# A hybrid decoder block: last down-projection step by token halves, the memset of the sums moved, residual in three pieces, other banks for the memory values

## The reference, cut to what matters

```python
x = x + rmsnorm(merged @ w_o[l], g_post_mix[l])
h2 = rmsnorm(x, g_pre_ffn[l])
u = causal_dwconv(h2 @ w_up[l], conv_w[l], conv_b[l])      # 2 x 5632 columns, 3 taps over the tokens
u_gate, u_val = jnp.split(u, 2, axis=-1)
f = (jax.nn.gelu(u_gate, approximate=True) * u_val) @ w_down[l]
x = x + rmsnorm(f, g_post_ffn[l])                          # rmsnorm: v * rsqrt(mean(v*v) + 1e-6) * g
```

## Time and profile before

| | |
|---|---|
| median of 3 runs | 1752.44 us |
| the profiled execution | 1752.13 us |
| its span, first to last instruction | 1749.8 us |
| granted TensorE clock, mean | 0.998 of full speed |
| PE / DVE / ACT / POOL busy | 98% / 63% / 47% / 2% |
| bytes over the DMA queues | 327.77 MB, 187 GB/s |

### The profile page before, as it was taken

One profiled execution on the slowest core, in us unless ns is written; L12 is line 12 of the kernel. 1 busy time (PEld: TensorE's weight loads), 2 busy tenths in 40 slices (PEclk: granted clock), 3 DMA queues, 4 the chain that ended last, 5 costly groups with the idle time before them and its releaser, 6 DMA issues.

```text
span 1749.8 us, 26499 instructions
## 1 busy us (share of the span) xinstructions
PE 1710.7 (98%) x9645; PEld 1499.8 (86%) x9645; DVE 1095.5 (63%) x1426; ACT 817.0 (47%) x1107; POOL 42.9 (2%) x49
## 2 busy tenths in 40 slices
PE   6999999999999999999999999999999999999997
PEld 6998999999878888888888788888888888888885
DVE  5644557666566454564565667776676676676676
ACT  5433335444434434434444555455454455454453
POOL 0000000000031000000000100000000000000000
PEclk9999999999999999999999999999999999999999
DMA  8755458545465666666647555666666666666663
GB/s 260 228 176 185 143 147 275 159 144 156 150 199 165 191 197 192 208 201 193 190 166 252 182 166 188 191 190 187 190 193 192 189 190 188 191 192 191 193 188 115
DMA packets 246146, 327.77 MB, mean 187 GB/s; under 512 B 12727, under 2 KB 167464, under 8 KB 245544
## 3 DMA queue, kind: packets, MB, share of 16 engines
q1 hardware_dynamic: 246056, 326.47, 60.2%
HBM read 321.71 MB, written 3.67 MB: 186 GB/s over the span
## 4 chain that ended last, share of the span: by engine, by line
PE 94%; DVE 2%; DMA 2%; ACT 1%; issue 0%; SPq 0%; DVEq 0%; POOL 0%; ACTq 0%; POOLq 0%
PE bank L1295 18%; PE bank L1285 15%; PE bank L1286 15%; PE bank L1287 15%; PE bank L1299 9%; PE bank L1259 4%; PE bank L1261 4%; PE bank L1260 4%; PE bank L1272 1%; PE bank L1274 1%; PE bank L1273 1%; DMA wraw<-in_w_in 1%; DVE wlo L795 1%; ACT whi L527 1%; DMA wraw<-in_w_o 0%
## 5 line engine op out<-in xcount | busy, mean ns | idle before, releaser
L795 DVE TENSOR_TENSOR wlo<-wraw,whi 128x1024 fp32r<-128x1024 f32 x588 | 722.6, 1234 | 481.5 <-ACT whi L527 479.5
L527 ACT ACTIVATE whi<-wraw 128x1024 fp32r<-128x1024 f32 x588 | 621.4, 1060 | 719.2 <-PE bank L1287 395.0
L1295 PE MATMUL bank<-hx,whi 128*128 128x512 f32 x1376 | 344.5, 392 | 0.0
L1295 PEld LDWEIGHTS bank<-hx,whi 128*128 128x128 f32 x1376 | 248.0, 189 | 44.9
L1299 PEld LDWEIGHTS bank<-hx,wlo 128*128 128x128 f32 x1376 | 187.7, 190 | 13.4
L1299 PE MATMUL bank<-hx,wlo 128*128 128x256 f32 x1376 | 191.9, 282 | 0.0
L1285 PE MATMUL bank<-whi,hx 128*128 128x512 f32 x448 | 175.7, 392 | 0.0
L1287 PE MATMUL bank<-whi,hx 128*128 128x512 f32 x448 | 174.4, 389 | 0.0
L1286 PE MATMUL bank<-wlo,hx 128*128 128x512 f32 x448 | 174.3, 389 | 0.0
L1285 PE MATMUL bank<-whi,r_hi 128*128 128x512 f32 x416 | 162.2, 390 | 0.0
L1286 PE MATMUL bank<-wlo,r_hi 128*128 128x512 f32 x416 | 162.0, 389 | 0.0
(11 more groups left out here) (241 smaller groups left out, 2071.6 us busy)
## 6 DMA issues: line engine op xcount, KB each, us to landing
wraw<-in_w_in SPq DMA_DIRECT2D x200, 512.0 KB, 3.6
wraw<-in_w_up SPq DMA_DIRECT2D x176, 512.0 KB, 4.4
wraw<-in_w_down SPq DMA_DIRECT2D x88, 512.0 KB, 4.2
wraw<-in_w_mem_kv SPq DMA_DIRECT2D x32, 512.0 KB, 4.3
wraw<-in_w_o SPq DMA_DIRECT2D x32, 512.0 KB, 4.4
wraw<-in_w_br_mem SPq DMA_DIRECT2D x16, 512.0 KB, 4.1
wraw<-in_w_br_nsa SPq DMA_DIRECT2D x16, 512.0 KB, 4.5
wraw<-in_w_br_ret SPq DMA_DIRECT2D x16, 512.0 KB, 4.3
```

The source lines that it names most:

```text
L527: nc.scalar.activation(whi[:, c], wraw[:, c], ACT.Copy).then_inc(hi_done, 1)
L795: V.tensor_tensor(wlo[:, c], wraw[:, c], whi[:, c].bitcast(F32), ALU.subtract).then_inc(lo_done, 1)
L1295: T.matmul(ps[UP_PAIRS[j][t]][:, :], whi[:, c, k, t * P:(t + 1) * P], hx[:, :, k0 + k, :], start=first and k == 0, stop=False, skip_group_ ...
```

## The change

- The last down step goes by token halves: all 2048 columns of tokens 0 to 127 in the banks 0, 1, 6, 7, then those of tokens 128 to 255 in 2, 3, 4, 5. All eight weight chunks have to stay, so the last four go to the buffers `m_hi` and `m_lo`, which are free by then (`kept`). VectorE's additions, ScalarE's squares, the mean, power, residual sum and stores follow half by half; the power is of one column each.
- GpSimd's memset of `M` waits for the last split tile of the norm instead of for `x2`.
- The residual ahead of the norm is made and squared in pieces of 1024, 512 and 512 channels.
- "mv" uses bank pair (2, 7) first and (0, 1) second; group 0 waits for no pair, group 1 for what was emptied before the phase.
- In retention VectorE multiplies by the decay ahead of the first weight split instead of behind it.

```diff
+X2_PARTS = [(0, 1024), (1024, 1536), (1536, 2048)]
-OUT_PARTS = [(0, 0, 512), (0, 512, 1024), (1, 0, 1024), (1, 1024, 512), (0, 1536, 512), (1, 1536, 512)]
+OUT_PARTS = [(0, 0, 1024), (0, 1024, 1024), (1, 0, 512), (1, 512, 512), (1, 1024, 512), (1, 1536, 512)]
-NEW_PAIRS = ("mv", "rg")
+LAST_BANKS = ((0, 1, 6, 7), (2, 3, 4, 5))
...
+        def kept(buf, c):
+            return (m_hi, m_lo)[buf].rearrange("p k s -> p (k s)")[:, 1024 * c:1024 * (c + 1)]
...                                             # GpSimd
-            pool.wait_ge(s_x2, 2 * TT)
+            pool.wait_ge(s_trl, 2 * KT)
             nc.gpsimd.memset(arena[:, A_M:A_M + 4096], 0.0).then_inc(s_f0, 1)
-            rstd(6)
+            half_rstd(6, 0)
+            half_rstd(7, 1)
...                                             # ScalarE, hi()
+                if isinstance(q, int) and q == DN_LAST:
+                    nc.scalar.activation(kept(0, c), wraw[:, c].rearrange("p k n -> p (k n)"), ACT.Copy).then_inc(hi_done, 1)
+                    return
...                                             # ScalarE, norm
             row_squares(1, 1)
+            row_squares(1, 2)
...                                             # ScalarE, last step
-            for g in range(4):
-                for t in range(TT):
-                    act.wait_ge(s_dn, 4 + 8 * (STEPS - 1) + 2 * g + t + 1)
+            for t in range(TT):
+                for g in range(4):
+                    act.wait_ge(s_dn, 4 + 8 * (STEPS - 1) + 4 * t + g + 1)
...                                             # VectorE, "mv"
-                ch.add(V.tensor_copy(by_head(A_MV + 1024 * i, 0), ps[PAIRS[i][0]][:, :]...))
-                dve.sem_inc(evac[i], 1)
+                ch.add(V.tensor_copy(by_head(A_MV + 1024 * i, 0), ps[PAIRS[1 - i][0]][:, :]...))
+                dve.sem_inc(evac[1 - i], 1)
...                                             # VectorE, retention
-                    ahead(q, (0,))
                     dve.wait_ge(r_i, r + 1)
                     ...                         # the two products with the decay
-                    ahead(q, (1,))
+                    ahead(q, (0, 1))
...                                             # VectorE, last step
+            ahead(Q0["dn"])
+            for t in range(TT):
+                for g in range(4):
+                    dve.wait_ge(s_dl, 4 * t + g + 1)
+                    f = M[:, t, 512 * g:512 * (g + 1)]
+                    V.tensor_tensor(f, ps[LAST_BANKS[t][g]][:, :], f, ALU.add).then_inc(s_dn, 1)
+                    if g:
                         times_gain(g - 1, t)
-            mean_square(4, 4, (s_sq, 16), lambda: [times_gain(3, t) for t in range(TT)], 6)
-            ch.wait()
-            for part in OUT_PARTS:
-                post(M, *part, s_fin)
+                dve.wait_ge(s_sq, 8 + 4 * t + 4)
+                half_square(t, 0, 4, 0)
+                times_gain(3, t)
+                ch.wait()
+                dve.wait_ge(s_rstd, 7 + t)
+                for part in OUT_PARTS:
+                    if part[0] == t:
+                        post(M, *part, s_fin)
...                                             # TensorE, group()
+                if phase == "mv":
+                    for b in range(2 * i):
+                        pe.wait_ge(evac[b], G0[phase] // 2)
...
+                pair = PAIRS[(i + (phase == "mv")) % 2]
...                                             # TensorE, last step
+            def last_down(q, s, u):
+                pe.wait_ge(s_al, s + 1)
+                for b in range(2):
+                    pe.wait_ge(evac[b], up_group(s + 1))
+                for t in range(TT):
+                    if t:
+                        pe.wait_ge(s_dn, 8 * s + 4)
+                    for g in range(4):
+                        o = ps[LAST_BANKS[t][g]][:, :]
+                        for c in range(2):
+                            n = 4 * (g // 2) + 2 * (g % 2) + c
+                            if t == 0:
+                                pe.wait_ge(lo_done, 4 * q + n + 1)
+                            ...                 # chunks 0 to 3 from whi, wlo, chunks 4 to 7 from kept
+                            for k in range(2):
+                                ...
+                                T.matmul(o, xh, vh[:, k, :], start=c == 0 and k == 0, stop=False)
+                                T.matmul(o, xh, vl[:, k, :], start=False, stop=False)
+                                e = T.matmul(o, xl, vh[:, k, :], start=False, stop=c == 1 and k == 1)
+                        e.then_inc(s_dl, 1)
```

More of the change, by code:

```diff
@@ L695, in row_squares @@
             def row_squares(t, h):
[L697 to L699 removed]
+                act.wait_ge(s_x2, 3 * t + h + 1)
+                own = slice(*X2_PARTS[h])
+                nc.scalar.activation((r_hi, r_lo)[t][:, own], X[:, t, own], ACT.Square, accum_out=sq[:, 1, t, h:h + 1]).then_inc(s_ssq, 1)
             def half_hi(t, pairs):
@@ L711, in _ @@
             group_squares(3, 0)
-            row_squares(0, 0)
-            row_squares(0, 1)
+            for h in range(3):
+                row_squares(0, h)
             act.wait_ge(pe_done, 4 * WO_LAST + 4)
@@ L790, in lo @@
                 dve.wait_ge(hi_done, 4 * q + (c + 1))
-                if isinstance(q, int) and q == WO_LAST:
+                if isinstance(q, int) and q == DN_LAST:
+                    V.tensor_tensor(kept(1, c), wraw[:, c].rearrange("p k n -> p (k n)"), kept(0, c).bitcast(F32),
+                                    ALU.subtract).then_inc(lo_done, 1)
+                elif isinstance(q, int) and q == WO_LAST:
                     V.tensor_tensor(held(1, c), wraw[:, c].rearrange("p k n -> p (k n)"), held(0, c).bitcast(F32),
@@ L1131, in _ @@
             dve.wait_ge(s_rstd, 3)
[L1132 to L1135, removed]
+            for h in range(3):
+                residual(0, h)
+            dve.wait_ge(s_ssq, 2 * 2 * TT + 3)
+            half_square(0, 6, 3, 1)
             dve.wait_ge(s_rstd, 4)
@@ L1147, in _ @@
             residual(1, 1)
+            residual(1, 2)
             half_lo(0, (4, 5))
-            dve.wait_ge(s_ssq, 2 * 2 * TT + 4)
-            half_square(1, 6, 2, 1)
+            dve.wait_ge(s_ssq, 2 * 2 * TT + 6)
+            half_square(1, 6, 3, 1)
             half_lo(0, (6, 7))
@@ L1386, in group @@
             def group(q, chunks, i, phase, x_, between={}, tiles_ready=None):
-                for b in range(2):
-                    if b == i % 2 or (i == 0 and phase in NEW_PAIRS):
-                        pe.wait_ge(evac[b], G0[phase] // 2 + i // 2)
+                if phase == "mv":
+                    for b in range(2 * i):
+                        pe.wait_ge(evac[b], G0[phase] // 2)
+                else:
+                    for b in range(2):
+                        if b == i % 2 or (i == 0 and phase == "rg"):
+                            pe.wait_ge(evac[b], G0[phase] // 2 + i // 2)
+                pair = PAIRS[(i + (phase == "mv")) % 2]
                 for c in range(chunks):
@@ L1394, in group @@
                         pe.wait_ge(tiles_ready[0], tiles_ready[1] + c + 1)
-                    chunk_w(q + c // 4, c % 4, PAIRS[i % 2], *x_, 2 * c, c == 0, c == chunks - 1)
+                    chunk_w(q + c // 4, c % 4, pair, *x_, 2 * c, c == 0, c == chunks - 1)
                     if c in between:
@@ L1694, in _ @@
                 down(q + 4, s, s % 2)
-            down(Q0["dn"], STEPS - 1, 0)
+            last_down(Q0["dn"], STEPS - 1, 0)
 def constants():
```

29 lines of the change are left out of this document (15 added, 14 removed).

## The result

| | before | after |
|---|---|---|
| median of the runs beside each other | 1752.61 us (4 runs, 1752.35 to 1753.65) | 1743.04 us (4 runs, 1742.29 to 1743.83) |
| the profiled execution | 1752.13 us | 1743.83 us |
| its span | 1749.8 us | 1741.4 us |

The ratio is 0.9941, 95% interval 0.9928 to 0.9953: 9.6 us less.

A forecast was written before the change was run, and what follows sets the result against it. TensorE, busy 98% of the span, was taken as the bound, leaving only its waits and the tail. Gains of 1.0 + 2.3 + 1.05 + 3.6 = 7.95 us off 1752.13, plus 0.3 for the median, gave 1744.5 us; range 1743.2 to 1747.9.

The forecast's parts named there:

- rival A: Behind the norm: the memset holds up the weight splits, TensorE loses 3.3 us, 1747.8 us; chance 0.1.
- Rival B: Last down step: VectorE becomes the bound, 0.3 to 1.5 us of tail gain lost, about 1745.5 us; chance 0.15.
- D: Last down step, first pass: a TensorE pause drops its clock to 1.2 GHz, 10.9 us more, 1755.4 us; chance 0.02.
- stalls in retention: Retention outputs: with the decay first, TensorE's waits go; 1.8 + 3 x 0.16 = 2.3 us gained.
- the stores' backlog: Tail: the transfer backlog of some 0.4 us at the end goes; 0.25 us of it counted as gain.
- "mv": Start of the memory values: the other bank pair spares group 0 its wait for a copy; 1.0 us gained.
- rival C: "mv" and retention: the waits only move, because another ends right behind; 1747.8 us; chance 0.04.
- Norm: Norm ahead of the up-projection: removed memset stall, 1.15 us, less 0.1 for the residual pieces; 1.05 us gained.
- The loss of 0.1 for the third piece: Residual ahead of the norm: two squares of 512 replace one of 1024, costing 0.1 us on the second half.
- The memset beside the splits: Behind the norm: the moved memset does not delay the weight splits beside it; 0 taken, bounds 0 to 3.3 us.
- The last step: Last down step: last chunk split by 1723.7 to 1724.8, TensorE stall taken as 0, VectorE just in time.
- The tail: Behind TensorE's last matmul: earlier start of sums 0.95, fewer sums 2.4, stores 0.25; 3.6 us gained.

The follow-up runs named there:

- e4: The kernel before with only the other bank pair for the memory values of "mv"; 1751.77 us, ratio 0.9992.
- e6: The kernel before with half of each compression-weight transfer left out and the other bank pair for the memory values; 1752.4 us, ratio 0.9993.
- e5: The kernel before with half of each compression-weight transfer left out; 1752.6 us, ratio 0.9997.
- e13: The kernel before with half of every weight transfer around the compression left out, plus the other bank pair for the memory values; 1749.05 us, ratio 0.9979.
- e2: The kernel before with only the retention decay moved ahead of the first weight split; 1749.65 us, ratio 0.9981.
- e11: The changed kernel with the residual ahead of the norm in two pieces again; 1741.88 us (one run).
- e7: The changed kernel with GpSimd's memset replaced by a multiplication by zero, which also reads SBUF; 1755.04 us (one run).
- e1: The kernel before with only the last down step by token halves; 1748.95 us, ratio 0.9973.
- e8: The changed kernel with the first token half's stores held back until the second half's first sum; 1746.55 us (one run).
- e9: The changed kernel unaltered, measured once more; 1743.92 us, ratio 0.9943.
- e12: The kernel before with half of every weight transfer around the compression left out (compression weights and `w_in` chunks); 1750.57 us, ratio 0.9984.

## Why the prediction came out a little too high

The waits that the prediction named went, and rivals A, B and D fell. What failed are sizes. Two terms were priced too low: the stalls in retention (2.3 us, measured 2.97) and the stores' backlog in the tail (0.25 us, measured 0.85). The range, too, had no term for executions that differ by 2 us in one stretch.

- **"mv", 1.0 us.** The wait went: the gap shrank from 1.21 to 0.12 us, and to the first query score the edit gave 1.23 us. How much of it lasts is open. The argument against rival C, that roundings, splits and transfers follow TensorE and so move up with it, has no term for how long the transfers take, and in the compression stretch they are late. Behind it the profiled pair is level (0.02 us), e4 0.34 ahead of before, e6 level with e5, and with light transfers e13 keeps all. But these are single executions in a stretch that varies by 2 us from one to the next, and before's was the shortest of those without the edit and with whole transfers. The means of ten runs, 1.4 us less in e4 and 0.9 in e6, speak for most of the 1.0 us, without showing it.
- **Retention, 2.3 us.** Measured 2.97 and 2.84 (e2). The cost of one stall was taken as idle time plus 0.16. Besides this the first product took 0.70 us instead of 0.59 in all four heads, although the 0.70 stood in the prediction's rows. The second product then starts 0.10 us later, 0.4 us in all. The stall of the fourth head, which shows no idle time, cost 0.2 more. These 0.6 us the prediction left out; it had named the fourth head in its bounds only.
- **Norm, 1.05 us.** Measured 1.24. The loss of 0.1 for the third piece did not come (e11); ahead of the norm 0.20 us were lost between the two checkpoints, for a reason that no run shows.
- **The memset beside the splits, 0.** Right, now shown from both sides. A subtraction of two SBUF tiles is not held up by a GpSimd instruction that only writes (3.50 us for three, beside the memset and without), and is by one that reads (11.93 us, e7). This is what the Trainium skill ("SBUF — State Buffer", section "Who interferes with whom") states, and both halves of its rule agree with the trace; by it rival A could have had less than its 0.1.
- **The last step.** The weights came as forecast. TensorE ends 4.02 us sooner than before, and so counted the last transfer is issued at the same point (1713.67, before: 1717.69) and the last chunk is split at 1720.22 + 4.02 = 1724.24, inside 1723.7 to 1724.8. VectorE was not late: from there to the end of its multiplication ahead of the last addition (1732.12) it took 11.9 us instead of 12.7, with waits of 1.08 us in it instead of 1.5. Rival B fell by 0.90 us of idle time, as did D.
- **The tail, 3.6 us.** Measured 4.38, and 4.3 in e1. Start of the sums: 1.14 us sooner instead of 0.95, the power being 0.92 us long and starting 1.90 after the addition. The sums: 2.39 of 2.4. The mis-sized term is the stores' backlog, 0.25 us in the prediction and 0.85 measured (3.56 us from the last sum's end to the end before, 2.71 after). It was read from the rate in one stretch of 2 us. The bytes still to be moved at the end of the last sum differ by 0.26 MB, which at some 380 GB/s is 0.7 us of the 0.85 (an estimate from the rates under e8).

With the sizes of the profiled pair the sum is 0.90 - 0.88 + 2.97 - 0.20 + 1.24 - 0.01 + 4.38 = 8.40 us, as measured, instead of 7.95. That explains 0.45 of the 1.5 us. The other 1.0 is how the profiled executions stand to the medians. The prediction added 0.3 us for this, from the kernel before. But after's was the slowest of four, 0.8 us above its median (two runs lie at 1742.3, two at 1743.8), and before's was below all runs beside it.

The medians lie 9.57 us apart. If the 1.23 us of "mv" last on average, the sum is 1.23 + 2.97 - 0.20 + 1.24 - 0.01 + 4.38 = 9.61. The fit speaks for this reading, but no run shows it term by term. That the time lies just outside the range and not just inside is chance: e9's median, 1743.92 us for the same kernel, lies inside it.

The same stretch is the likely source of much of the spread between runs. From the first query score to L1566 or its like, the eleven profiled executions with whole transfers took 153.5 to 155.5 us, and the two with all transfers halved 151.9 both. The runs of before beside e12 spread over 2.9 us, those of e12 over 1.5, and nine of e13's ten over 0.7. The range of the prediction had no term for this; its lower end was the sum of the upper ends of the gains.

One thing stays open: how much of the "mv" gain is left on average. Over the eight profiled executions that have the edit, without e13, L1566 or its like is reached at 322.2 us on average, over the five without it, without e12, at 322.9. But each group scatters by 2 us or more. A profile of many executions of the same two kernels would be needed.

## What to carry to other kernels

Before adding up removed waits, look between each and the end for a stretch where the transfers are full and the leading buffers run dry. Here such a stretch differs by 2 us from execution to execution, more than the gains of "mv" and of the norm, so one profiled pair could not tell whether a gain ahead of it lasts; ten runs of each, or a run with lighter transfers, say more. When two timelines are compared, take off how far apart they already were ahead of the edit. Price a stall by the starts of the matmuls on both sides of it and the length of the first one behind, not by the idle time alone. In a tail, look at when the first byte of the output can leave: storing half of the result under the last matmuls was worth more than the shorter arithmetic suggested.

## What the runs showed of the hardware that was not expected

- The first of the retention output products (two matmuls of 256 columns) took 0.70 us before the change and 0.59 after it, and the next one started 0.10 us sooner (0.43 instead of 0.53 us later).
- In the compression stretch a chunk of 512 KB took 4.1 us from the issue of its transfer to its rounding, half a chunk 2.7 us (e12).
- A GpSimd multiplication by a constant over 128 x 4096 words took 10.55 us beside VectorE's subtractions, a memset of the same size 3.54 us.
- In and behind an idle time of 8.39 us the granted clock was 0.50 for 8 us, the last 3 of them with TensorE at work again, and 1.00 from 5 us after its restart (e7).
- The power of one column took 0.92 us beside a multiplication of two SBUF tiles on VectorE, 0.54 without.
